# Modulation products woven into a neighbourhood-attention phase, and weights scaled on VectorE before the next maximum

## The reference, cut to what matters

```python
def adaln(cond, w_mod_l, b_mod_l, n_chunks):
    m = jax.nn.silu(cond) @ w_mod_l[:, :n_chunks * D_MODEL] + b_mod_l[:n_chunks * D_MODEL]
    return jnp.split(m, n_chunks, axis=-1)

h = modulate(x, sh1, sc1)                     # layer_norm(x) * (1 + sc1) + sh1
u = h @ w_in_l
o_b = neighbourhood_latent(q_b, k_b, v_b, kc_b, vc_b, nat_bias[l])
o = jnp.concatenate([o_a, o_b, o_c], axis=-1) @ w_out[l]
x = layer_norm(ALPHA * x + g1 * o, ln1_g, ln1_b)
h2 = modulate(x, sh2, sc2)
x = layer_norm(ALPHA * x + g2 * ec_moe(h2, ...), ln2_g, ln2_b)   # 16 experts, 64 tokens each by top-k
```

## Time and profile before

| | |
|---|---|
| median of 3 runs | 2793.3 us (2789.22 to 2798.05) |
| profiled execution | 2786.06 us |
| its span | 2784.2 us |
| mean granted TensorE clock | 0.986 |
| busy: TensorE, VectorE, ScalarE, GpSimd | 94%, 38%, 25%, 7% |
| first block, layers 0 and 1 | 0 to about 905 us |
| second block, layer 0: mixer, experts | about 905 to 1327, to 1870 us |
| second block, layer 1: mixer, experts, end | to 2286, to 2762, to 2784 us |

### The profile page before, as it was taken

One profiled execution on the slowest core, in us unless ns is written; L12 is line 12 of the kernel. 1 busy time (PEld: TensorE's weight loads), 2 busy tenths in 40 slices (PEclk: granted clock), 3 DMA queues, 4 the chain that ended last, 5 costly groups with the idle time before them and its releaser, 6 DMA issues. The chain is left out here.

```text
span 2784.2 us, 44403 instructions
## 1 busy us (share of the span) xinstructions
PE 2620.4 (94%) x17914; PEld 1421.7 (51%) x17914; DVE 1069.5 (38%) x2323; ACT 698.4 (25%) x1835; POOL 207.4 (7%) x253
## 2 busy tenths in 40 slices
PE   8999999999999999898999999999999989999897
PEld 5565656565657766555434444436766543322222
DVE  3023340023447853656122222237752552332234
ACT  2125311134412443422111111203442320000000
POOL 2000020000001010011000000001010110000000
PEclk9999999999999999999999999999999999999999
DMA  8343634443632011025999999972012249999996
GB/s 246 88 123 90 181 88 121 121 124 78 205 75 55 31 29 31 31 91 217 380 377 399 399 395 396 404 210 63 16 29 91 106 184 398 404 410 411 404 413 272
DMA packets 268627, 570.06 MB, mean 205 GB/s; under 512 B 12416, under 2 KB 203200, under 8 KB 219328
## 3 DMA queue, kind: packets, MB, share of 16 engines
q1 hardware_dynamic: 256512, 528.69, 52.0%
q0 software_dynamic: 11824, 39.18, 5.3%
q10 hardware_dynamic: 144, 0.14, 0.0%
HBM read 551.53 MB, written 16.42 MB: 204 GB/s over the span
## 5 line engine op out<-in xcount | busy, mean ns | idle before, releaser
L510 PE MATMUL ps<-turned,ring 128*128 128x512 f32 (+1 forms) x880 | 327.6, 530 | 0.0
L510 PEld LDWEIGHTS ps<-turned,ring 128*128 128x128 f32 x880 | 166.4, 190 | 153.9 <-issue 147.7
L818 PE MATMUL ps<-ring,mixT 128*128 128x512 f32 x512 | 223.6, 594 | 0.8 <-DVE mixT L1993 0.8
L1423 ACT ACTIVATE work<-ps 128x512 f32<-128x512 f32 x32 | 19.1, 598 | 687.7 <-PE ps L1325 404.7
L2034 ACT ACTIVATE probsT<-ps 128x512 f32<-128x512 f32 (+3 forms) x280 | 120.5, 456 | 230.2 <-PE ps L646 143.8
L1967 DVE TENSOR_REDUCE col<-ps 128x1 f32<-128x256 f32 (+4 forms) x136 | 79.0, 581 | 257.5 <-PE ps L604 224.5
L604 PE MATMUL ps<-kz,qz 96*128 96x512 f32 (+3 forms) x320 | 135.9, 507 | 22.6 <-ACT probs_v L2021 10.0
L2021 ACT ACTIVATE probs_v<-ps,col 128x256 f32<-128x256 f32 (+5 forms) x216 | 136.5, 632 | 79.6 <-DVE col L1967 56.9
L818 PEld LDWEIGHTS ps<-ring,mixT 128*128 128x128 f32 x512 | 95.8, 190 | 114.6 <-issue 113.4
L553 PE MATMUL ps<-turned,ring 128*128 128x512 f32 (+1 forms) x352 | 152.8, 562 | 1.0 <-DMA ring<-in_w_in 1.0
L632 PE MATMUL ps<-const,probs_v 128*128 128x128 f32 x752 | 122.8, 280 | 17.0 <-DVE probs_v L1985 13.9
(11 more groups left out here) (327 smaller groups left out, 3976.4 us busy)
## 6 DMA issues: line engine op xcount, KB each, us to landing
ring<-in_w_gate SPq DMA_DIRECT2D x64, 1024.0 KB, 19.8
mixT<-in_w_up SPq DMA_DIRECT2D x64, 1024.0 KB, 14.1
ring<-in_w_mod SPq DMA_DIRECT2D x96, 512.0 KB, 5.6
ring<-in_w_up SPq DMA_DIRECT2D x48, 1024.0 KB
ring<-in_w_in SPq DMA_DIRECT2D x82, 512.0 KB, 6.4
turned<-in_w_gate SPq DMA_DIRECT2D x32, 1024.0 KB, 17.9
mixcT<-in_w_down SPq DMA_DIRECT2D x32, 1024.0 KB
probs_v<-in_w_down SPq DMA_DIRECT2D x32, 1024.0 KB
```

The source lines that it names most:

```text
L510: mm = nc.tensor.matmul(ps[:, b, 0:n], w[:, k, :], rhs[:, k, 0:n], start=(k == 0), stop=(k == KD - 1))
L818: mm = nc.tensor.matmul(ps[:, b, :], lhs[:, k, tl * P:(tl + 1) * P], w, start=(k == 0), stop=(k == KD - 1))
```

## The change

1. **Modulations.** The first block keeps seven products in each layer (steps 0 and 2 of `fox`, `sb` and `mla`, and the tail). Products 7 to 10 move into `nb` as a generator (`mod_products`) that `weave` calls twice in each step, after the scores and at the step's end, for one block k (four matmuls) each time. Product 11 takes the place of `pe_busy(3)` in the mixer's tail. Their weights are loaded behind the `nb` weights, before and after those of the output projection.
2. **`nb` on VectorE.** Bias of unit i, then reciprocal and scaling of unit i − 1, then the maximum of unit i.
3. **Scores over 128 partitions** in every kind but `mla`.
4. **`dve_half_stats`.** In the tails of the first block and of the mixer, the statistics of the last tile's first half are taken as soon as that half is there.
5. **`act_top_values`.** Copies of the top values go from VectorE (L1846, L1848, L1851) to ScalarE.
6. **`keep_residual`** of the mixer's last tile goes behind the first gather on GpSimd.
7. **The end of the program.** Sums go to bank pairs 0, 6, 4, 0; residuals are added before the last product; the statistics of tiles 1 to 3 are taken on ScalarE.

```diff
-        mod_order = [(l, j) for l in range(DEPTH) for j in range(12)]
+        FIRST_MODS, NB_MODS, LAST_MOD = 7, range(7, 11), 11
+        mod_order = [(l, j) for l in range(DEPTH) for j in range(FIRST_MODS)]
...
-            q = (QC if kind in ("ca", "cb") else qz)[0:KROWS, hh, t * P:(t + 1) * P]
+            R = slice(0, KROWS if kind == "mla" else P)
+            q = (QC if kind in ("ca", "cb") else qz)[R, hh, t * P:(t + 1) * P]
...
-        MOD_STEPS = {"fox": (0, 2, 17), "sb": (0, 2, 15), "mla": (0, 2, 17), "mem": (0, 4)}
+        MOD_STEPS = {"fox": (0, 2), "sb": (0, 2), "mla": (0, 2)}
...
+        def mod_products(l):
+
+            def products(fill):
...
+                for j in NB_MODS:
+                    w = [slot(nc.tensor, ("mod", l, 4 * j + q)) for q in range(4)]
+                    job = ("mod", l, j)
+                    yield "not before", 1
+                    b = open_job(nc.tensor, job, keep=True)
+                    for k in range(KD):
+                        for q in range(4):
+                            mm = nc.tensor.matmul(ps[32 * q:32 * q + 32, b, 0:P], cond[:, k, :], w[q][:, k, :],
+                                                  start=(k == 0), stop=(k == KD - 1), skip_group_check=True)
...
+                        yield "ns", 280
+                        if k == 3 and j > NB_MODS[0]:
+                            turn(j - 1)
+                yield "not before", fill["place"][1] + 2
+                turn(NB_MODS[-1])
...
+                    + [x for j in NB_MODS for x in mod_slots(l, j)]
+                    + [(w1(2 + l, "wo", k), w_rows(a["w_out_2"], l, k)) for k in range(KD)]
+                    + mod_slots(l, LAST_MOD))
...
-            pe_softmax(pe, ("nb", l, 0))
+            pe_softmax(pe, ("nb", l, 0), mod_products(l), 400)
...
                     if i == n:
-                        pe_busy(pe, 3)
+                        pe_mod(pe, (l, LAST_MOD))
...
+            pe.wait_ge(*at("top_values", l))
...
+            b = (0, 6, 4, 0)[t] if l > 0 else sum_banks(l, t)[0]
...
             gather(0)
+            keep_residual(l, mixer_tiles(l)[-1])
...
+                if half == 0:
+                    dve.wait_ge(*(at("evac_dve", job) if kind == "first" else at("dve_step", ("res", st, t, 0))))
+                    dve_half_stats(dve, (st, t), res(t))
...
+                biased = i < len(us) and us[i][0][0] == "nb"
+                if biased:
+                    bias(us[i])
+                elif i < len(us):
                     top(us[i])
                 if 1 <= i <= len(us):
                     norm(us[i - 1])
+                if biased:
+                    top(us[i])
...
+            nc.scalar.activation(spare, total, ACT.Copy, accum_out=end_col(1, t)).then_inc(*done("act_step", ("sum", t)))
...
+            nc.scalar.activation(end_col(0, t), end_col(1, t), ACT.Copy, scale=-1.0 / D).then_inc(*done("act_step", ("mean", t)))
...
+            nc.scalar.activation(spare, total, ACT.Square, bias=end_col(0, t),
+                                 accum_out=end_col(2, t)).then_inc(*done("act_step", ("squares", t)))
...
+                if i == n:
+                    act_mod(act, (l, LAST_MOD))
...
+                if i == n + 1:
+                    dve_mod(dve, (l, LAST_MOD))
```

More of the change, by code:

```diff
@@ L332, in close_job, with close_job_turned @@
             closing[job] = place
+        def close_job_turned(job, place):
+            closed.setdefault(place, []).append(job)
         def bank_of_open(job):
@@ L600, in pe_scores @@
                     parts.append((unit16, causal16, w - P))
-                parts += [(q, KC[0:KROWS, part, c * P:(c + 1) * P], w + c * P) for c in range(NC)]
+                parts += [(q, KC[R, part, c * P:(c + 1) * P], w + c * P) for c in range(NC)]
             for lhs, rhs, o in parts:
@@ L740, in pe_mod_turn, with turn @@
             nc.tensor.transpose(ps[:, b, 0:P], modrow[:, :], ident).then_inc(*done("job_done", job))
-        MODS = 3
         def mods_at(ph, i, delay):
             kind, l = ph[0], ph[1]
[L749 to L754, removed]
+            if kind in MOD_STEPS:
+                for n, step in enumerate(MOD_STEPS[kind]):
+                    if i - delay == step:
+                        return l, 2 * list(MOD_STEPS).index(kind) + n
             return None
-        MOD_STEPS = {"fox": (0, 2, 17), "sb": (0, 2, 15), "mla": (0, 2, 17), "mem": (0, 4)}
+        MOD_STEPS = {"fox": (0, 2), "sb": (0, 2), "mla": (0, 2)}
         def mod_of_tail(l):
-            return mod_order[MODS * 4 * (l + 1) - 1]
+            return l, FIRST_MODS - 1
+        def mod_products(l):
+            def products(fill):
+                def turn(j):
+                    pe_mod_turn(nc.tensor, (l, j))
+                    close_job_turned(("modT", l, j), fill["place"])
+                for j in NB_MODS:
[7 more added lines that the diff above has]
+                                                  start=(k == 0), stop=(k == KD - 1), skip_group_check=True)
+                        if k == KD - 1:
+                            mm.then_inc(*done("job_done", job))
+                            for q in range(4):
+                                last_use(("mod", l, 4 * j + q), job)
+                            close_job(job, fill["place"])
+                        yield "ns", 280
[3 more added lines that the diff above has]
+                turn(NB_MODS[-1])
+            return products
         def pe_head(pe, st, t):
@@ L1362, in body @@
                     gate(e + 1, 1 - odd)
+                last = l > 0 and is_number(e) and e == EXPERTS - 1
+                if last:
+                    residual(0, 0)
                 pe.wait_ge(*nth("hid", l, e))
@@ L1380, in body @@
                     turn_xs(e + 2)
+                if last:
+                    residual(0, 1)
                 pe.wait_ge(*nth("hidT", l, e))
@@ L1944, in act_moe_out @@
                 if n + 1 < len(tiles):
-                    act_root(act, (st, tiles[n + 1]), LN_EPS_2)
+                    if last:
+                        act_end_stats(act, tiles[n + 1])
+                    else:
+                        act_root(act, (st, tiles[n + 1]), LN_EPS_2)
                 if not last and not ctile(t):
@@ L1950, in dve_softmax, with bias @@
             us = joined(ph)
+            def bias(u):
+                dve.wait_ge(*at("scores", u))
+                (_, l, _), t, hh = u
+                dve.wait_ge(*at("bias_ready", (l, hh)))
+                o = (7 - 2 * t) * 64
+                logits = s_psum(u)[:, 0:SEQ]
+                nc.vector.tensor_tensor(logits, logits, bias_of(hh)[:, o:o + SEQ],
+                                        ALU.add).then_inc(*done("dve_step", ("nb", u)))
             def top(u):
@@ L1998, in dve_softmax @@
             lag = lag_of(ph)
-            for i in range(len(us) + lag + 2):
-                if i < len(us):
+            for i in range(len(us) + lag + 3):
+                biased = i < len(us) and us[i][0][0] == "nb"
+                if biased:
+                    bias(us[i])
+                elif i < len(us):
                     top(us[i])
@@ L2827, in _ @@
                         ml, j = next(mods)
-                        for q in range(4):
-                            load_slot(sp_, ("mod", ml, 4 * j + q), w_cols(a["w_mod_2"], ml, (4 * j + q) * P))
+                        for key, part in mod_slots(ml, j):
+                            load_slot(sp_, key, part)
                     else:
```

178 lines of the change are left out of this document (122 added, 56 removed).

## The result

The changed kernel takes 2827.1 us (median of 4 runs, 2821.91 to 2833.13) for 2791.84 of the kernel before: a ratio of 1.0128, with a 95% interval of 1.011 to 1.0146. It is 35 us slower where 13 us faster was forecast. The profiled execution has a span of 2820.1 us against 2784.2, and a mean granted clock of 0.987 against 0.986.

A forecast was written before the change was run, and what follows sets the result against it. TensorE, busy for 94% of the span, was taken as the bound. Terms −16.7 + 11 − 2.6 − 2.6 − 0.3 − 1.6 = −12.8 us, off the median 2793.3, gave 2780.5 us; range 2768 to 2792.

The forecast's parts named there:

- Products that leave the first block: First block: five products fewer in each layer's `fox`, `sb`, `mla` and `mem` save 8.35 us a layer, −16.7 in both.
- Products woven into `nb`: In `nb`, four woven pieces a pair of units lengthen the phase by 5.5 us a layer, +11 in both.
- Once the idle 0.70 is filled TensorE bounds the pair: In `nb`, a pair takes TensorE's work 5.63 plus 1.58 us for four pieces: 7.21, or +0.88.
- the four rivals: Pieces hide, 2769.5 us (0.22); array drains, 2793.2 (0.18); clock falls in `nb`, 2815 (0.06); transfers delay first expert, 2790.5 (0.04).
- the clock: Rival: in `nb`, thin pieces between weight changes bring the granted clock to 0.60, costing 35 us: 2815 us; chance 0.06.
- VectorE's order: In `nb`, transposes start 0.96 us earlier, removing the pair's idle 0.70, which the pieces also fill; counted once, extra 0.
- the maximum has slack: In `nb`, the maximum comes 0.77 us later at no cost, VectorE's work being about 5.1 of 7.2 us a pair.
- Scores over 128 rows: Attention scores: contracting over 128 rows instead of 96 changes no instruction's duration; no term, 0.
- Tails: Tails: half statistics −2.6 us, the mixer's GpSimd residual moved behind the gather −2.6, copies to ScalarE −0.3.
- Transfers: Before the experts: 4 MB of expert weights load later, taking 10 us, covered by SyncE's 22 idle us: 0.
- the fourth rival: Before the experts: the 4 MB of later-loaded weights delay the first expert by 10 us: 2790.5 us; chance 0.04.
- The end: Program's end: statistics on ScalarE at 3.6 us a tile against VectorE's 3.96, and an earlier start, save 1.6 us.

The follow-up runs named there:

- Experiment 1: Changed kernel with VectorE copying finished pairs out and taking in transposed modulations first in its `nb` step, not last: 2774.19 us, 0.9919 of the kernel before.
- experiment 9: Changed kernel with only the copy of a finished pair first in VectorE's `nb` step, the transposed modulation still last: 2784.21 us, 0.9978 of the kernel before.
- experiment 7: Kernel before with only its scores contracted over 128 partitions, except in `mla`: 2787.0 us over 10 runs, 0.9982 of the kernel before.
- experiment 4: Kernel before with only VectorE's new order in `nb`: 2781.74 us, 0.9945 of the kernel before.
- experiment 6: Experiment 1 with VectorE's old order, the maximum before the scaling: 2774.14 us, 0.994 of the kernel before.
- experiment 2: Changed kernel with VectorE's old order in `nb` (bias, maximum, scaling), weaving kept: 2830.11 us, 1.0124 of the kernel before.
- experiment 3: Changed kernel without weaving, products 7 to 10 back in the first block: 2767.85 us, 0.9899 of the kernel before.
- experiment 5: Experiment 1 with both blocks of a step woven in one piece at the step's end: 2766.96 us, 0.9913 of the kernel before.
- experiment 8: Experiment 3 with SyncE's queue in layer 1 waiting for the first expert's gathered rows before loading the last 4 MB of expert weights: 2768.82 us, 0.9933.

## Why the prediction was wrong

The direction was wrong and the time lies outside the range. By its own steps:

- **Products that leave the first block**, −16.7: mechanism right, size low. Measured −21.8 (12 in layer 0, 10 in layer 1). `mem` gave 5.0 in each layer where 3.5 was taken out of at most 5.0; `fox` and `sb` together 4.7 and 3.1 where 2.65 was; `mla` 2.0 for 2.2.
- **Products woven into `nb`**, +11: this is the step that failed. "Once the idle 0.70 is filled TensorE bounds the pair" added up matmuls and asked of each piece what it costs, not what its job must wait for when it opens. The prediction did not follow the PSUM bank that a product holds over four steps, nor where in VectorE's step the bank beside it is emptied. That wait had no term, and none of the four rivals had it: the one on the slower side was the clock, which did fall, but behind the waits. Measured +65.7. Experiment 1 takes 52.9 of it away, experiment 9 shows the 8.6 of it that belong to the modulation; what stays is 6.9 and 5.9 in the two layers, near the +5.5 of the forecast. That nearness is partly luck: four pieces cost 1.82 us and not 1.58, and with the transposes eight pairs give +9.5 for the +7.0; the rest of the phase is 3.6 us shorter for the 1.5, of which 1.3 are the 128 rows (experiment 7).
- **VectorE's order**, "counted once": right. Alone it gives 4.9 and 5.0 us (experiment 4), with the weaving under 1 us (experiment 6). The sentence that the maximum has slack held too (experiment 2).
- **Scores over 128 rows**, 0: wrong by about 5 us (experiment 7; the interval says 1.7 to 8), of which the profile shows 1.9 us in part 1 of `wa` of layer 1 and 1.3 us in each `nb`, both where a stretch at 1.2 GHz is shorter or gone. The term was looked for in the duration of one instruction, where there is none.
- **Tails**, −5.5: about a third. The two mixers' tails are 4.0 us longer; without the 6.0 us that the gathers lost (next point) they are 2.0 shorter. In the mixer the half statistics gave their 0.6; in the first block of layer 0 the stretch from the last matmul of the output projection to the next scores is 107.9 us in both kernels, so nothing. L1806 went from 1.52 to 0.23 as said, but of the 1.9 us of both edits 1.4 reached the gather, since TensorE then waited 0.98 us for the router's input.
- **Transfers**, "that covers them: 0": wrong. The 22 idle microseconds hid the expert weights, but the gather lay beside the late ones, and its first matmul came 2.6 us later in layer 1 and 3.4 in layer 0 (4.6 to 8.0). It was the fourth rival, at 6.0 of its 10 us. In layer 1 it isn't the woven products' weights alone: without weaving (experiment 3) the gather takes 8.0 us there, and 4.2 in layer 0.
- **The end**, −1.6: measured −1.7, but not by the terms of the sum. ScalarE took 3.0 us a tile, not 3.6, and began 0.9 us before VectorE's turn; the last tile took 1.1 us longer from its first statistic to the end (6.3 for 5.2), which had no term.
- Not foreseen: −5.4 in the experts of layer 0. A wait of 3.76 us of L1325 at 1404.3 before is gone in the changed kernel. It stays in experiments 4 and 7 and is gone in 1 and 3, so neither the order nor the 128 rows alone removes it, nor does it take the weaving; which of the other edits does was not tried. The stretch itself varies between the traces (644.3 us in experiment 3, 648.4 in experiment 1), so not all of the 5.4 need be the change's.

What was said to show the prediction wrong, `nb` more than 10 us a layer longer, did.

Open is what makes the clock fall behind these waits, and what such stretches would cost by themselves: with the waits gone none was left in `nb`.

## What to carry to other kernels

A piece of work put into idle time costs what it must wait for when it opens, besides its own duration: write down which buffer it takes, how long it holds it, and at which point of another engine's step the buffer beside it is emptied. An engine's step should begin with what frees a buffer and end with what nobody waits for; moving one copy of 0.28 us (once in two steps) from the end of a step to its start was worth about 43 us here (experiment 9). And small matmuls of another column width are best left together: the same four products cost 11 to 12 us a layer in 32 pieces and 5.8 in four.

## What the runs showed of the hardware

A change of the array's column width costs 0.09 to 0.15 us, on either side of a piece (experiments 1 and 5). Zero rows are not without effect: contracting over 128 partitions instead of 96 leaves the duration of the scores as it was (1.12 and 1.13 us for two records of 512 columns) but shortens the stretch at 1.2 GHz in the window attention of layer 1 from 13.7 to 6.8 us, 1.9 us of time (experiment 7). An indirect gather of 64 rows lands 3.8 to 3.9 us after its issue at a DMA share of 0.24 to 0.35, and 8.0 us at 1.02 (experiment 8).
